# Turning cached keys in 32x32 blocks on VectorE instead of in 128x128 tiles on TensorE

## The reference

```python
ATT_GROUPS = ((128, 1), (512, 4), (2048, 16))      # window, dilation

def band_attention_sample(q, k_all, v_all, n_past, dil, band, slopes):
    t = q.shape[1]
    j = jnp.arange(band + 1)
    idx = n_past + jnp.arange(t)[:, None] - j[None, :] * dil
    ...
    kg = k_all[:, idx].astype(jnp.float32)
    vg = v_all[:, idx].astype(jnp.float32)
    sc = jnp.einsum('bthd,btjhd->bhtj', q.astype(jnp.float32), kg) * (HEAD_DIM ** -0.5)
    ...
    p = jnp.exp(sc - lse[..., None])
    o = jnp.einsum('bhtj,btjhd->bthd', p, vg)
```

## Time and profile before

| | us |
|---|---|
| median of 3 runs | 1924.23 (1922.79 to 1927.62) |
| the profiled execution | 1922.89 |
| its span, first to last instruction | 1921.0 |
| PE busy | 1880.7 (98%) |
| PEld busy | 1283.0 (67%) |
| DVE busy | 638.9 (33%) |
| ACT busy | 460.9 (24%) |
| POOL busy | 193.7 (10%) |

### The profile page before, as it was taken

One profiled execution on the slowest core, in us unless ns is written; L12 is line 12 of the kernel. 1 busy time (PEld: TensorE's weight loads), 2 busy tenths in 40 slices (PEclk: granted clock), 3 DMA queues, 4 the chain that ended last, 5 costly groups with the idle time before them and its releaser, 6 DMA issues.

```text
span 1921.0 us, 44783 instructions
## 1 busy us (share of the span) xinstructions
PE 1880.7 (98%) x20479; PEld 1283.0 (67%) x20480; DVE 638.9 (33%) x1081; ACT 460.9 (24%) x688; POOL 193.7 (10%) x260
## 2 busy tenths in 40 slices
PE   7999999999999999999989999999999999999998
PEld 7998877999999998877974353534435353443534
DVE  4466543754435456643541010110201011020101
ACT  4434432444334434543331000000000000000000
POOL 2114100234303113200100000000000000000000
PEclk9999999999999999999999999999999999999999
DMA  8543799655445443689637999999999999999996
GB/s 275 163 136 130 229 305 348 215 156 173 161 168 172 156 154 130 196 289 343 210 141 263 416 391 397 409 380 411 374 415 385 403 407 384 409 372 415 385 407 259
DMA packets 212398, 553.81 MB, mean 288 GB/s; under 512 B 11482, under 2 KB 107914, under 8 KB 195680
## 3 DMA queue, kind: packets, MB, share of 16 engines
q1 hardware_dynamic: 207680, 541.67, 76.3%
q0 software_dynamic: 3248, 9.18, 1.4%
q10 hardware_dynamic: 1280, 0.06, 0.0%
HBM read 543.46 MB, written 7.77 MB: 287 GB/s over the span
## 4 chain that ended last, share of the span: by engine, by line
PE 94%; DVE 2%; DMA 2%; ACT 1%; SPq 1%; issue 1%; DVEq 0%; POOL 0%; ACTq 0%; POOLq 0%
PE psum L949 89%; PE psum L957 5%; DMA high_part<-in_const_a 1%; DMA low_part<-in_w_branch_attn 1%; DVE w_split L1824 1%; SPq L830 1%; ACT w_split L1541 0%; DVE low_part L2323 0%; DVE low_part L1817 0%; DVE low_part L1936 0%; DVE high_part L1941 0%; SPq L814 0%; ACT low_part L1511 0%; DVE high_part L1861 0%; DVE xn_split L1836 0%
## 5 line engine op out<-in xcount | busy, mean ns | idle before, releaser
L949 PE MATMUL psum<-low_part 128*32 128x512 f32 (+3 forms) x6926 | 677.7, 528 | 6.8 <-ACT low_part L1511 4.7
L949 PEld LDWEIGHTS psum<-xn_split,w_split 128*128 128x128 f32 x3744 | 504.1, 189 | 42.5 <-issue 29.1
L949 PE MATMUL psum<-xn_split,w_split 128*128 128x288 f32 x3744 | 521.0, 298 | 5.4 <-DMA high_part<-in_const_a 4.0
L949 PEld LDWEIGHTS psum<-low_part 128*32 128x32 f32 (+2 forms) x6926 | 239.9, 114 | 398.7 <-issue 391.0
L949 PE MATMUL psum<-low_part,high_part 128*32 128x256 f32 (+3 forms) x6636 | 343.6, 359 | 3.3 <-DVE low_part L1817 2.3
L1824 DVE TENSOR_TENSOR w_split<-low_part,w_split 128x2048 fp32r<-128x2048 f32 x104 | 238.7, 2295 | 265.2 <-ACT w_split L1541 265.0
L949 PEld LDWEIGHTS psum<-low_part,high_part 128*32 128x32 f32 (+1 forms) x6636 | 217.3, 111 | 129.0 <-issue 14.7
L1541 ACT ACTIVATE w_split<-low_part 128x2048 fp32r<-128x2048 f32 x104 | 199.0, 1914 | 262.6 <-PE psum L949 220.7
L2335 DVE TENSOR_TENSOR low_part<-high_part,psum 128x384 f32<-128x384 f32 (+1 forms) x48 | 29.8, 621 | 426.2 <-PE psum L949 423.8
L1788 ACT ACTIVATE high_part<-psum 128x384 f32<-128x384 f32 (+1 forms) x48 | 25.9, 544 | 395.0 <-PE psum L949 394.1
L957 PE MATMUL psum<-high_part,low_part 128*128 128x128 f32 (+2 forms) x839 | 108.6, 279 | 10.5 <-DMA low_part<-in_x_sample 7.4
(11 more groups left out here) (159 smaller groups left out, 942.6 us busy)
## 6 DMA issues: line engine op xcount, KB each, us to landing
low_part<-in_we_down SPq DMA_DIRECT2D x112, 1024.0 KB, 8.5
low_part<-in_cache_kv_g SPq DMA_DIRECT2D x72, 1024.0 KB, 5.8
low_part<-in_we_gate SPq DMA_DIRECT2D x64, 1024.0 KB, 8.2
low_part<-in_we_up SPq DMA_DIRECT2D x64, 1024.0 KB, 8.4
low_part<-in_w_in SPq DMA_DIRECT2D x55, 1024.0 KB, 5.1
low_part<-in_we_gate SPq DMA_DIRECT2D x64, 768.0 KB, 7.7
low_part<-in_we_up SPq DMA_DIRECT2D x64, 768.0 KB, 6.9
low_part<-in_w_dense SPq DMA_DIRECT2D x33, 1024.0 KB, 5.3
```

What stands on the lines that cost most here:

```text
L949: signal(e.matmul(out, lhsT, rhs, start=start, stop=stop, skip_group_check=mixed), inc)
```

## The change

16 of a layer's 18 key chunks (all but the group-0 chunk of each half) are loaded in four pieces. Piece `i` holds the 128 floats of two heads (2i and 2i + 1), 512 bytes of a 2048-byte row, and goes to partitions 32i to 32i + 31, where each partition holds four keys of each sequence. DVE then turns the whole chunk in blocks of 32x32 in one instruction (`turn_keys`), into one of two buffers of four tiles (`keysT`, the same memory as `cacheT`). After that each group of 32 partitions holds half a head's dimensions of two heads in four column groups, and the score product for column group `x` reads its 128 keys as four pieces of 32. The stationary queries are placed to match (`place_quarters`): 16 copies of 32 partitions x 32 elements for each half, now on ACT; POOL keeps the rows of group 0 and the new keys for both halves (`place_queries`). DVE releases the ring slot when the chunk is turned.

The order changes too (`KEY_STEPS`): each of the nine unit steps has two key steps, half 0 is scored from the third unit step to the seventh, half 1's group-0 chunk is turned in the seventh, four chunks of it are scored in the last two, and the last five follow. The first gate's weight chunk is sent before the last two key chunks (`GATE_AHEAD`). PE's wait for the tables moves behind two column tiles and the sum of squares. The core of the diff:

```diff
+KEY_SLOTS = 2 * (NU + 1)
+KEYS_FROM = (2, 12)
+def key_steps():
+    out = [[] for _ in range(KEY_SLOTS + 1)]
+    for half, first in enumerate(KEYS_FROM):
+        for n in range(BH):
+            out[first + n // 2].append(("turn", half, n))
+        for n in range(NQ):
+            out[min(first + 2 + n, KEY_SLOTS)].append(("score", half, n))
+    return out
...
+QUARTERED = [c for c, n in CACHE_ORDER.items() if n < HB * NQ and n % NQ]
...
+        keysT = [[view(ws_at + 2 * CH * free_half[L] + CH * i, BH, 4, 4, QUAD) for i in range(2)] for L in range(LAYERS)]
...
+        def place_quarters(e, half):
+
+            src = qT.rearrange("p (g j) t -> p g j t", g=G)[:, 1:G, :, SEQ + 16 * half:SEQ + 16 * (half + 1)]
             for j in range(J):
...
+                one = view(q_one_at, 2 * J * BH * DS * 32)[QUAD * j:QUAD * (j + 1), :]
+                for x in range(4):
+                    e.activation(strided(one, x * BH * DS * 32 + 2 * j + x // 2, (J * BH * DS * 32, 2), (128, BH), (32 + H, DS)),
+                                 src[QUAD * x:QUAD * (x + 1), :, j, :].rearrange("p g (b t) -> p g b t", b=BH), ACT.Copy)\
+                        .then_inc(quarters_placed.sem, 1)
...
+                    if c in QUARTERED:
+                        dst = view(slot(c), BH, 4, 128)
+                        src = src.rearrange("(k s) b (i d) -> i s b k d", k=4, i=4)
+                        send(L, c, [(dst[QUAD * i:QUAD * (i + 1)], src[i]) for i in range(4)])
...
-                e.wait_ge(tables_loaded, 16)
                 for n in range(36):
                     if n == 2:
                         ssq(L, S, 0)
+                        e.wait_ge(tables_loaded, 16)
                     column_tile(column_job(n), PG + n)
...
-                    for n in range(n0, n0 + BH):
-                        S.wait_read(e, ("kT", half, n))
+                    if n0:
+                        e.wait_ge(keys_turned.sem, keys_turned.at(L, half * (NQ - 1) + q % NQ))
+                    else:
+                        for n in range(BH):
+                            S.wait_read(e, ("kT", half, n))
...
+                            keys = keysT[L][q % 2][:, b, :, j, :] if n0 else cacheT[L][(BH * q + b) % CACHE_SLOTS][:, j, :]
...
+                    if v == 1:
+                        e.wait_ge(zeroed.sem, zeroed.at(L, 1))
+                        place_quarters(e, 0)
+                    if v == NU - 2:
+                        S.wait_full(e, ("ss", 0))
+                        place_quarters(e, 1)
...
+                def turn_keys(q):
+
+                    half, n = q // NQ, q % NQ
+                    c = CACHE_CHUNK[q]
+                    wait_chunk(e, L, c)
+                    e.wait_ge(split_used, L * NW_LAYER + W_MERGE)
+                    wait_cache_slot(e, L, S, BH * q)
+                    e.transpose(keysT[L][q % 2].rearrange("p b k x s -> p (b k x s)"), view(slot(c), CH))\
+                        .then_inc(keys_turned.sem, 1)
...
+                        for q in TURNED_AHEAD[2 * v + he]:
+                            turn_keys(q)
```

More of the change, by code:

```diff
@@ L199, with turned_ahead @@
 CACHE_SLOTS = 8
[L202 to L215, removed]
+KEY_SLOTS = 2 * (NU + 1)
[8 more added lines that the diff above has]
+    return out
+KEY_STEPS = key_steps()
+def turned_ahead():
+    out = [[] for _ in range(KEY_SLOTS)]
+    for at, steps in enumerate(KEY_STEPS[:KEY_SLOTS]):
+        out[at - 1] += [HB_NQ for kind, half, n in steps if kind == "score" and n for HB_NQ in (half * NQ + n,)]
+    out[KEY_SLOTS - 1].append(KEY_STEPS[KEY_SLOTS][0][1] * NQ + KEY_STEPS[KEY_SLOTS][0][2])
+    return out
+TURNED_AHEAD = turned_ahead()
+LAST_TURNED = range(TURNED_AHEAD[-1][-1] + 1, HB * NQ)
 SCORES_AT = 32
 K_HOMES = 4
-MAX_AT, EXP_AT, SCALE_AT, PT_AT = 3, 6, 9, 14
+PT_AFTER = 15
 EX0_GATE = 4
@@ L251, in branch_tiles, with key_jobs @@
     return [(name, 2 * i + x) for x in range(2) for name in ("pb", "ab")]
+def key_jobs(at):
+    out = []
+    for kind, half, n in KEY_STEPS[at]:
+        if kind == "turn":
+            out.append((("kT", half, n), UKPOOL[half]))
+        elif n == 0:
+            out.append((("ss", half), (SS_BANKS[half],)))
+    return out
 def section_attention():
@@ L267, in section_attention @@
             js += [(("S", v + 1, he), UPOOL) for he in range(2)]
-        js += [(("kT", 0, m), UKPOOL) for m in step_tiles(v, 0)]
+        js += key_jobs(2 * v)
         if v >= 1:
             js.append((("O", v - 1), UPOOL))
-        js += [(("kT", 0, m), UKPOOL) for m in step_tiles(v, 1)]
+        js += key_jobs(2 * v + 1)
         if v < NU:
             js += [(("T", v, he), UPOOL) for he in range(2)]
[L274 to L280, removed]
+    js += [(("pt", 0), KPOOL), (("pn", 0), KPOOL)]
+    js += [(("OS", half), (O_BANKS[half],)) for half in range(HB)]
     for gate in range(KT):
@@ L1233, in attention @@
                         values(v - 1)
-                    for m in step_tiles(v, 1):
-                        cache_step(m)
+                    key_steps_at(2 * v + 1)
                     if v < NU:
                         turn_probs(v)
-                for m in range(REST, HB * NT + LAG):
-                    cache_step(m)
+                key_steps_at(KEY_SLOTS)
                 def gather_heads(half):
@@ L1622, in attention, with cache_copies @@
                             copy(S, job, v_tok[0:count, tt, g, :], S.ps(job)[0:count])
-                def cache_copy(m):
-                    if copied_by_act(m):
-                        wait_cache_slot(e, L, S, m)
-                        copy(S, ("kT", m // NT, m % NT), cacheT[L][m % CACHE_SLOTS], S.ps(("kT", m // NT, m % NT))
-                             .rearrange("p (j m) -> p j m", j=J))
+                def cache_copies(at):
+                    for kind, half, n in KEY_STEPS[at]:
+                        if kind == "turn":
+                            m = half * NT + n
+                            wait_cache_slot(e, L, S, m)
+                            copy(S, ("kT", half, n), cacheT[L][m % CACHE_SLOTS],
+                                 S.ps(("kT", half, n)).rearrange("p (j m) -> p j m", j=J))
                 scale(0)
```

125 lines of the change are left out of this document (57 added, 68 removed).

## The result

The changed kernel takes 1931.6 us (median), the kernel before beside it 1925.7 us: ratio 1.0031, 95% interval 1.0022 to 1.0041. It is slower by 0.3%, where 1908.8 us were forecast; the value lies above the range. The profiled execution has 1933.57 us and a span of 1931.7 us, against 1922.89 and 1921.0 us.

What follows compares the result with a forecast made beforehand. PE, busy 98% of the span, was taken as the bound; 5.6 us from the table wait plus 2 x 4.9 us from the layers gave 15.4 us gain, 1908.8 us forecast, range 1891 to 1928 us.

Steps and rivals of the forecast that it cites:

- second block: PE's new-key products (2.76 us) and one score chunk after the second half's placements: placed at about 227.1, done to 231 us.
- the drop charged: One fall of PE's clock a layer after a placement pause: 1.5 us, with 0 and 3 us as ends.
- Table wait: At program start, moving PE's wait removes a 4.03 us pause and a 1.53 us slow stretch: 5.6 us, once.
- DVE's turn and pace: In the key part, a 128x2048 turn takes 2.28 us and DVE sets the units' pace at 7.85 us each.
- The queries' places: ACT's 16 small placements per half, ahead of the first key scores: 2.6 us as upper value, lower end near zero.
- warning sign: If ACT's small placement operations take over 0.3 us each, the forecast is wrong.
- The clock: PE's granted clock falls after a placement pause, as at the start: one drop of 1.5 us a layer.
- The loads: Twelve quarter-row key chunks and two full ones on the SP queue stay hidden while a chunk takes below 5.2 us.
- c: Time of one quarter-row key chunk's load: 3.8 us taken, ends 3.07 and 7.2 us.
- the quick case: Rival, 14%: no stall at the placements, no clock drop; 9.0 us a layer, 23.6 us in all, 1900 us.
- The gates' stretch: The gates with the cached values keep their 80.9 us; 26 loads of 1 MB fit with 79.8 us.
- The slower one: Rival, 8%: small packets cost like large ones, 7.2 us a chunk, 17.9 us later in each layer, 1954 us.

Runs made afterwards that it cites:

- experiment 1: The kernel before with only PE's wait for the tables moved behind the sum of squares: 1920.2 us, ratio 0.9978.
- Experiment 7: Changed kernel with needless PE work before its waits for the placements: 36 and 42 turns 1922.2 us; as many products 1927.5 us; 18 and 21 products 1920.8 us.
- experiments 3 and 6: 3: changed kernel, key chunks loaded as whole rows, one transfer each, 1934.0 us; 6: changed kernel, eight transfers a chunk, order 0, 2, 1, 3, 1934.1 us.
- experiment 2: Changed kernel with the quarter rows of the queries placed by GpSimd instead of ACT: 1920.4 us, ratio 0.9983.
- experiment 4: Changed kernel with GpSimd placing the quarter rows and key chunks loaded as whole rows by one transfer each: 1909.5 us, ratio 0.9914.

## Why the prediction was wrong

Measured from the first tile of layer 0 (171.60 us in the forecast's times, 166.55 us in the changed kernel), in us; unit 3 and 6 are the tiles that DVE biases in these unit steps, counted from 0:

| mark | forecast | measured | late by | added since the mark above |
|---|---|---|---|---|
| unit 3 on DVE | 21.3 | 26.7 | 5.4 | 5.4 |
| unit 6 on DVE | 44.8 | 50.5 | 5.7 | 0.3 |
| second block starts | 55.5 | 63.3 | 7.8 | 2.1 |
| it and its chunk done | 59.4 | 70.4 | 11.0 | 3.2 |
| first gate | 81.4 (82.9 with the drop charged) | 94.4 | 13.0 | 2.0 |

- **Table wait: right.** 5.6 us forecast, 5.05 us in the trace, 4.2 us by experiment 1, whose own trace keeps 3.6 us of it up to the first gate.
- **DVE's turn and pace: right.** 2.28 us forecast, 2.30 measured; 7.85 us a unit forecast, 7.60 measured for units 3 to 5; unit 6 then comes 8.6 us after unit 5, for the clock dips once more at 213 us.
- **The queries' places: the first step that failed.** "The upper value I take, 16 x 0.16 = 2.6 us" was no upper value: 4.4 us, 1.8 us more, twice a layer. The row it came from the earlier trace rows is an operation of 128x128 in a row of two; a small one between scattered places costs no less. The text set 0.3 us each as a warning sign, and 0.28 came. (GpSimd did not copy all of them before, as the text has it: DVE placed a quarter. Nothing hangs on that.)
- **The clock: the step that cost most.** "One such drop a layer, 1.5 us" was taken from the start. In place of the 1.5 us, each block behind a pause loses 7.17 - 3.84 = 3.3 us, 6.6 us a layer, and the chunk and values behind the second block, the last chunks and the first gate (5.14 us, where 3.45 is usual) run slow too. Experiment 7 shows that this is the clock, and that it isn't lost where no pause is left. With the placements, 3.6 + 6.6 us of the 13.0 are named; the rest may lie in the slow pieces around them (the chunk and values behind the second block take 1.75 us more than at full clock), but no experiment takes it apart.
- **The loads: c was wrong, and the conclusion came out right by luck.** A chunk was put at 3.8 us; at 210 GB/s its 1.05 MB take 5.0 us. The estimate by the Trainium skill ("SBUF — State Buffer", "Door 1: The DMA port swizzle"), 5.5 us, was nearer. The 5.0 us are under the 5.2 us up to which the forecast saw the loads hidden, and experiments 3 and 6 show them hidden in the changed kernel. But what hid them was a delay that the forecast didn't have: DVE's wait of 10.13 us for PE. Where that goes, in experiment 2, the first gate starts at 87.9 us with the same loads, and with whole rows (experiment 4) at 82.5 us, near the forecast's 81.4. So the limit of 5.2 us was too high: at the pace that was forecast the loads would have bound. The forecast's own price for the quick case, 1900 us, overlooked this.
- **The gates' stretch: right**, 80.9 us.

So 15.4 us were forecast as gain; the table wait gave 4 to 5, and each layer gave back some 5 us by the medians (6.6 and 7.1 us in the traces) instead of bringing 4.9. None of the rivals was what happened. The slower one named the loads; the mechanism that won was a wait taking the place of the turns, which the text priced but priced low, and without its echo in the clock.

## What to carry to other kernels

When a change makes the bounding engine wait, price the wait twice: the pause itself, at what small operations cost (count them, and take no large one's overlap as their upper end), and the work behind the pause at the lower clock, every time it happens (in the changed kernel behind all four pauses of 4.0 to 5.9 us). Put such small operations on an engine that has them done before they are asked for. And look for the resource that is hidden only by the wait you are about to remove: here the same edit of the loads was worth nothing before that, and 9 us after.

## What the runs showed of the hardware

- After pauses of 3.98 to 5.92 us the granted clock stayed at 0.50 for 8 to 11 us of PE work, which cost the first 56 products 3.3 us each time; after 4.03 us at the start the work behind lost only 1.5 us. Leftover pauses of 0.9 to 1.4 us cost the clock in five of eight places, and a wait of 2.37 us was followed by a fall in one trace (experiment 1) and by none in another (the kernel before).
- A 32x32 copy to other partitions starts every 0.28 us on ACT; 16 on GpSimd, with four waits among them, take 4.6 us. Neither is cheaper than the other.
- From 205 to 236 us, four transfers into a quarter of the partitions each move 201 GB/s per unit of DMA share, where transfers into all 128 partitions move some 325, and eighths in mixed order 250.
